# A decoder layer with 32 experts: 2 MB weight transfers, and residual rows gathered as input and as base of the result

## The reference, cut to what matters

```python
x  = x + merged @ w_out[l]                      # the residual rows, "x2" in the kernel
h2 = rms_norm(x, norm2_g[l])                    # x * rsqrt(mean(x*x) + EPS) * gain
# router: best of 4 groups, in that group the best 2 of 8 experts, with weights w
a  = xb @ w_gate[eid]; u = xb @ w_up[eid]       # xb: rows of h2 that chose the expert
y  = (silu(a) * u) @ w_down[eid]                # 1024 -> 512 -> 1024
out[token] = x[token] + sum over its two experts of w * y
```

## Time and profile before

| what | value |
|---|---|
| median of 3 runs | 1505.51 us (1505.3 to 1505.54) |
| the profiled execution, its own time | 1504.28 us |
| its span in the profile | 1502.3 us |
| PE / weight load of PE / DVE / ACT / POOL busy, share of span | 95 / 80 / 68 / 51 / 26% |
| granted clock of PE, mean | 0.988 |
| data moved | 282.68 MB |

### The profile page before, as it was taken

How to read it: one execution, slowest core, us unless ns; L and a number is a source line. 1 busy time by engine, 2 the same in 40 slices (tenths; PEclk the granted TensorE clock), 3 DMA queues, 4 the chain that set the end, 5 groups by cost and what they waited for, 6 DMA issues and landing times.

```text
span 1502.3 us, 19200 instructions
## 1 busy us (share of the span) xinstructions
PE 1431.3 (95%) x7296; PEld 1198.4 (80%) x7297; DVE 1015.5 (68%) x1433; ACT 768.6 (51%) x1091; POOL 387.9 (26%) x448
## 2 busy tenths in 40 slices
PE   5899999999999999999999969999999999999995
PEld 4788888888888788888888858888888787777784
DVE  6855655664664433434332876999999999999994
ACT  5643453453453322333232446767777777777772
POOL 2325325424424300000001421333332222222221
PEclk9999999999999999999999979999999999999998
DMA  7011010110210333453341469999999999999991
GB/s 227 13 43 45 17 43 11 51 42 2 60 43 1 85 84 89 122 144 85 84 189 57 169 234 377 362 373 376 375 378 375 374 367 364 367 370 368 365 347 49
DMA packets 129996, 282.68 MB, mean 188 GB/s; under 512 B 15728, under 2 KB 94704, under 8 KB 105328
## 3 DMA queue, kind: packets, MB, share of 16 engines
q1 hardware_dynamic: 119216, 264.31, 48.8%
q0 software_dynamic: 9216, 16.81, 4.5%
q10 hardware_dynamic: 1472, 0.32, 0.1%
HBM read 273.00 MB, written 25.17 MB: 198 GB/s over the span
## 4 chain that ended last, share of the span: by engine, by line
PE 72%; DMA 14%; DVE 6%; issue 2%; ACT 2%; POOL 2%; POOLq 0%; DVEq 0%; ACTq 0%
PE proj L105 14%; PE proj L107 14%; PE proj L106 13%; DMA w_slot<-in_w_up 9%; PE scores L105 5%; PE scores L107 5%; PE scores L106 5%; DMA w_slot<-in_w_gate 4%; PE outs L751 2%; PE scores L684 2%; DVE w_low L1703 2%; ACT w_high L1167 1%; PE turned L105 1%; PE turned L107 1%; PE turned L106 1%
## 5 line engine op out<-in xcount | busy, mean ns | idle before, releaser
L1703 DVE TENSOR_TENSOR w_low<-w_slot,w_high 128x2048 fp32r<-128x2048 f32 x192 | 434.4, 2285 | 11.1 <-ACT w_high L1167 10.0
L1167 ACT ACTIVATE w_high<-w_slot 128x2048 fp32r<-128x2048 f32 x190 | 359.6, 1914 | 106.7 <-DMA w_slot<-in_w_gate 40.8
L105 PE MATMUL proj<-w_high,xeH 128*128 128x512 f32 x512 | 206.2, 403 | 11.5 <-DVE w_low L1703 8.7
L107 PE MATMUL proj<-w_high,xeL 128*128 128x512 f32 x512 | 201.3, 393 | 0.0
L106 PE MATMUL proj<-w_low,xeH 128*128 128x512 f32 x512 | 201.2, 393 | 0.0
L1343 POOL DMA_INDIRECT out<-y,ids_rows x32 | 107.1, 3347 | 228.9 <-DVE y L1800 228.9
L105 PEld LDWEIGHTS proj<-w_high,xeH 128*128 128x128 f32 x512 | 97.2, 190 | 38.9 <-DVE w_low L1703 16.3
L975 ACT ACTIVATE wCH<-wC_in 128x1024 fp32r<-128x1024 f32 x48 | 47.6, 1052 | 154.4 <-DMA wC_in<-in_w_branch_b 154.4
L1398 DVE TENSOR_TENSOR wCL<-wC_in,wCH 128x1024 fp32r<-128x1024 f32 x48 | 56.9, 1237 | 91.3 <-ACT wCH L975 91.3
L107 PEld LDWEIGHTS proj<-w_high,xeL 128*128 128x128 f32 x512 | 97.1, 190 | 21.3
L1335 POOL DMA_INDIRECT xe<-h_rows,ids_rows x32 | 54.8, 1711 | 225.9 <-PE scores L562 213.4
(11 more groups left out here) (277 smaller groups left out, 3080.5 us busy)
## 6 DMA issues: line engine op xcount, KB each, us to landing
w_slot<-in_w_gate SPq DMA_DIRECT2D x64, 1024.0 KB, 21.1
w_slot<-in_w_up SPq DMA_DIRECT2D x64, 1024.0 KB, 22.2
w_slot<-in_w_down SPq DMA_DIRECT2D x64, 1024.0 KB, 21.1
wC_in<-in_w_in SPq DMA_DIRECT2D x32, 512.0 KB, 4.9
wB_in<-in_w_in SPq DMA_DIRECT2D x16, 512.0 KB, 6.4
wA_in<-in_w_in SPq DMA_DIRECT2D x12, 512.0 KB, 5.8
x_all<-in_x SPq DMA_DIRECT2D x4, 1024.0 KB, 8.7
wC_in<-in_w_branch_a SPq DMA_DIRECT2D x16, 256.0 KB, 5.6
```

The costliest lines, as they stand in the source:

```text
L105: pe.matmul(out, lh, rh, start=start, stop=False)
L107: return pe.matmul(out, ll, rh, start=False, stop=stop)
L1167: act.activation(w_high[slot][:], w_in6[slot][:], ACT.Copy).then_inc(S["w_split"], 1)
L1703: dve.tensor_tensor(w_low[slot][:], w_in6[slot][:], w_high[slot][:].bitcast(F32), ALU.subtract).then_inc(S["w_lows"], 1)
```

## The change

- Pieces c = 0, 1 are now the halves of gate, 2, 3 those of up. Two neighbouring pieces in slots (0,1), (4,5), (6,7) or (8,9) come by one 2 MB transfer, issued when both slots are used up, with one semaphore; slots 2 and 3 stay alone.
- The normalised rows are no longer made. x2 is stored twice, to a DRAM tensor and to the output; the experts gather x2 rows, into four buffers xe0 to xe3. After the transposes ACT applies the gain: eight activations of 128x128 with a scale per partition, into `xs`; then it rounds `xs` to xeH, and DVE subtracts in SBUF. 1/rms of a row is applied in silu (as scale) and in the row weight.
- The result is one instruction, y = product x weight + xe (residual row), in one buffer, and the scatter is a plain write. For a token's second expert the base must be the row as the first left it: DVE makes a second table `ids2_rows` (entries only for second experts), and POOL gathers these rows once more from the output (`gather_again`). y(e) waits for scatter e - 1, and from e = 4 for its second gather.
- The weight step is moved behind the first low halves (`weigh`) and grows from 7 to 15 DVE instructions; `weigh_rows` makes 96 columns for 32; silu(0) waits for three tables out of it.
- silu(e) waits for piece (e, 1) and no longer (e, 3); hid(e) waits for (e, 3).

```diff
+ALONE = (2, 3)
+def land_of(slot):
+    return f"w_land{slot if slot in ALONE else slot - slot % 2}"
...
+            def load_pair(q):
+                _, j, c = PIECES[q]
+                slot = q % N_SLOTS
+                if slot in ALONE:
+                    load_one(q)
+                    load_one(q + 1)
+                else:
+                    if q >= N_SLOTS:
+                        sp.wait_ge(S["w_used"], q - N_SLOTS + 2)
+                    sp.dma_start(w_pairs[slot][:, :, 0:2048], source(expert_at(j), c).rearrange("p (a b) -> p a b", a=2)
+                                 ).then_inc(S[land_of(slot)], DMA)
...
-            def x_high(value):
-                act.wait_ge(S["xeT_done"], value)
-                act.activation(xeH[:].rearrange("p a b -> p (a b)"), SC[:, 0, :], ACT.Copy).then_inc(S["xeH_done"], 1)
+            def x_scaled(turned, value, ks, count):
+                act.wait_ge(S[turned], value)
+                if count is not None:
+                    act.wait_ge(S["xeL_done"], count)
+                for k in ks:
+                    act.activation(xs[:, k, :], SC[:, 0, k * 128:(k + 1) * 128], ACT.Copy, scale=g2x[:, k:k + 1]).then_inc(S["xs_done"], 1)
+            def x_high(value, count=None):
+                x_scaled("xeT_done", value, range(8), count)
+                act.wait_ge(S["xs_done"], value * 8)
+                act.activation(xeH[:], xs[:], ACT.Copy).then_inc(S["xeH_done"], 1)
...
             def gate_silu(e):
-                act.wait_ge(S["w_used"], use_of(e, 3) + 1)
+                act.wait_ge(S["w_used"], use_of(e, 1) + 1)
                 act.wait_ge(S["hid_done"], e)
-                act.activation(silu[:], PROJ[0][:, :], ACT.Silu).then_inc(S["silu_done"], 1)
+                if e == 0:
+                    act.wait_ge(S["rows_weighed"], 3)
+                act.activation(silu[:], PROJ[0][:, :], ACT.Silu, scale=r_rows[:, expert_at(e):expert_at(e) + 1]).then_inc(S["silu_done"], 1)
...
-                if n == 0 and i >= 2:
-                    pool.wait_ge(S[f"h2_stored{i % 2}"], DMA * (i // 2))
-                pool.wait_ge(S["x2_done"], 8 * n + i + 1)
-                pool.tensor_tensor(h2[:, i % 2, cols], x2[:, i, cols], g2_row[:, cols], ALU.mult).then_inc(S["h2_gained"], 1)
...
+            for r in range(1, N_EXP + 1):
+                scatter_rows(r - 1)
+                if r + 3 < N_EXP:
+                    gather_rows(r + 3)
+                if N_GROUPS <= r + 1 < N_EXP:
+                    gather_again(r + 1)
...
             def rows_out(e):
                 dve.wait_ge(S["w_used"], use_of(e, 5) + 1)
...
-                dve.tensor_scalar(ys[e % 2][:], SC[:, 1, :], w_rows[:, expert_at(e):expert_at(e) + 1], None, ALU.mult
-                                  ).then_inc(S["y_out"], 1)
+                if e:
+                    dve.wait_ge(S["scattered"], DMA * e)
+                if e >= N_GROUPS:
+                    dve.wait_ge(S[f"again_landed{e % 2}"], DMA * ((e - N_GROUPS) // 2 + 1))
+                dve.scalar_tensor_tensor(y[:], SC[:, 1, :], w_rows[:, expert_at(e):expert_at(e) + 1], xe[e % 4][:], ALU.mult, ALU.add
+                                         ).then_inc(S["y_out"], 1)
```

More of the change, by code:

```diff
@@ L543, in _ @@
             sp.wait_ge(S["tables_done"], 2)
             def loads_again(n, e, b):
[L546 to L553, removed]
+                sp.wait_ge(S["scattered"], n * DMA + DMA * N_EXP)
@@ L554, in _ @@
+                for c in range(6):
+                    sp.dma_start(w_in6[BLOCK_SLOTS[c]][:], source(e, c)[:, c % 2 * 2048:c % 2 * 2048 + 2048]).then_inc(S["v_w"], DMA)
+            sp.wait_ge(S["scattered"], DMA * N_EXP)
             overflow(sp, loads_again)
-            sp.wait_ge(S["x2_stored"], N_TILES * DMA)
+            sp.wait_ge(S["out_stored"], N_TILES * DMA)
         def turn_rows(pe, src_rows, dst, step, n):
@@ L1187, in _ @@
             for half, turned, done in ((0, "x0_T", "x0_H"), (1, "xeT_done", "xeH_done")):
-                act.wait_ge(S[turned], 1)
-                act.activation(xeH[:, 4 * half:4 * half + 4, :].rearrange("p a b -> p (a b)"), bank(half), ACT.Copy
-                               ).then_inc(S[done], 1)
+                ks = slice(4 * half, 4 * half + 4)
+                x_scaled(turned, 1, range(4 * half, 4 * half + 4), None)
+                act.wait_ge(S["xs_done"], 4 * half + 4)
+                act.activation(xeH[:, ks, :], xs[:, ks, :], ACT.Copy).then_inc(S[done], 1)
             for c in (0, 1):
@@ L1213, in block_steps @@
                 act.wait_ge(S["w_used"], n * 6 + (6 * N_EXP + 4))
-                act.activation(silu[:], PROJ[0][:, :], ACT.Silu).then_inc(S["silu_done"], 1)
+                act.activation(silu[:], PROJ[0][:, :], ACT.Silu, scale=cur_r[:, 0:1]).then_inc(S["silu_done"], 1)
                 hid_high(n + (N_EXP + 1))
                 act.wait_ge(S["w_used"], n * 6 + (6 * N_EXP + 6))
-                act.activation(ys[0][:], SC[:, 1, :], ACT.Copy, scale=cur_w[:, 0:1]).then_inc(S["y_out"], 1)
-            for g in range(N_GROUPS):
-                act.wait_ge(S[f"scattered{g}"], DMA * (N_EXP // N_GROUPS))
+                act.activation(y[:], SC[:, 1, :], ACT.Copy, scale=cur_w[:, 0:1]).then_inc(S["y_out"], 1)
+            act.wait_ge(S["scattered"], DMA * N_EXP)
             overflow(act, block_steps)
@@ L1327, in _, with ids_of @@
             pool.wait_ge(S["lg_done"], 16)
[L1328 removed]
+            pool.memset(xe[0][:], 0.0).then_inc(S["xe_zero"], 1)
             pool.wait_ge(S["xe_zero"], 1)
[L1330 to L1331 removed]
+            pool.wait_ge(S["x2_stored"], N_TILES * DMA)
             pool.wait_ge(S["tables_done"], 1)
+            def ids_of(table, j):
+                return bass.IndirectOffsetOnAxis(ap=table[:, expert_at(j):expert_at(j) + 1], axis=0)
```

336 lines of the change are left out of this document (170 added, 166 removed).

## The result

The changed kernel is slower by a little: 1509.68 us, median of 8 runs (1507.09 to 1510.89), against 1505.20 for the kernel before beside it (8 runs, 1503.29 to 1506.73). Ratio 1.0031, 95% interval 1.0022 to 1.0041. The forecast was 1500 and faster.

What follows compares the result with a forecast made beforehand. Late experts were taken as bound by weight loads, above PE's 17.77 us; afterwards an ACT-DVE chain at 18.1. Terms -5.4 - 3.8 + 4.9 - 1.2 = -5.5 us gave 1498.8 profiled, 1500 median; range 1496 to 1504, with rivals 1488 to 1510.

Steps and rivals of the forecast that it cites:

- Part 2: 2 MB weight transfers: fewer issues count nothing; landing allowance falls from about 11 to 8 us, and just holds.
- Part 3: Expert loop, chain from turned rows over ACT's gains to xeL: period 18.1 us against 18.28, -5.4 us over 30 experts.
- Part 1: DMA work per expert: plain scatter outweighs second gathers, queue 58.2 us for 67.6, DMA-bound cost 18.06 to 18.36 from 18.65.
- rival C: Late experts: DMA engines still bind, at 18.65 us per expert, 8.5 us above the forecast, 1508.5 us; chance 0.14.
- Rival D: Weight loads: larger transfers make DMA so fast that no load is late; alone brings nothing more; no chance given.
- Part 4: Other waits in the loop, y for the previous scatter and POOL's second gathers: all hidden, nothing added.
- Part 5: Before the experts: without POOL's gain products DVE's conversions and picks run faster; -3.8 us (0 to -5).
- Part 6: Expert 0: gains before its first products, and silu(0) waiting for the row tables, cost +4.9 us (3 to 7).
- Part 7: End of kernel: the last scatter, without read and addition, lands 1.2 us sooner (0 to 1.5).

Runs made afterwards that it cites:

- a1: Changed kernel with the high half of piece (e+1, 1) put ahead of the next rows' gains on ACT: 1507.86 us, ratio 1.0018.
- a3: Changed kernel without the second gathers and without the waits for them: 1501.58 us, ratio 0.9976.
- a2: Changed kernel with every piece a 1 MB transfer again, issued when its own slot is used up: 1503.19 us, ratio 0.9991.
- a4: Changed kernel with an expert's rows spread over the partitions, first 64 places to even ones, others to odd: 1502.00 us, ratio 0.9983.
- b1: Kernel before with the scatters as plain writes, the addition left out: 1487.59 us, ratio 0.9885.
- b2: Kernel before with an expert's rows spread over the partitions, first 64 places to even ones, others to odd: 1488.29 us, ratio 0.9893.
- b3: b2 with the last two pieces' high halves ahead of silu(31) on ACT and low(31, 4) ahead of y(30) on DVE: 1482.44 us, ratio 0.9859.
- a8: Changed kernel with two 128x512 products per tile put back on POOL, into unused memory: 1509.86 us, ratio 1.0036.

## Why the prediction was wrong

The forecast for the span was -5.5 us, the profiled executions differ by +5.7. The 11.2 us between them, by its steps:

| step | forecast | came | missed |
|---|---|---|---|
| loop (parts 1 to 4) | -5.4 | +0.6 (iteration 1 to 30) | 6.0 |
| before the experts and expert 0 (5, 6) | +1.1 | +4.1 | 3.0 |
| end (7) | -1.2 | +1.0 | 2.2 |

The loop's 6.0 us are 4.8 of late periods (part 2), 0.7 for 18.12 where 18.10 stood, and 0.5 because the forecast counted a thirtieth iteration that lies behind the last turning. No single step explains the whole: without the late periods after would stand near 1504.9 us (1509.7 - 4.8), still not at 1500.

**Part 3 was right**, to 0.02 us a period: 18.12 for 18.10. a1 shows that it was this chain.

**Part 2 is the step that failed most**: "it just holds". The allowance was sized well: 19.1 us to landing where it binds, 11.0 at first, the 8 that I took. What used it up was the DMA work, taken as an average of 18.36 at most for all experts. The second gathers are not spread evenly: the first four experts have none, later ones ever more, as the order runs through each group from its first expert to its last. In after the queue of gathers and scatters moved 1.74 MB in the first four periods from 929 us, 2.38 MB in 1074 to 1146 and 3.02 MB in 1292 to 1364; in a3 the last of these is 2.25. The median landing of the 2 MB transfers grew accordingly, by 0.8 us from the first four periods to the next (10.0 to 10.8) and by 2.1 us between the stretches 1219 to 1291 and 1292 to 1364 (14.7 to 16.8). Work that rises to the end meets a buffer that is nearly spent; 4.8 us were lost in five periods. The 2 MB transfers, which I counted at nothing but 3 us of allowance, had a part in it: with 1 MB transfers (a2) the same work was never late. So had the second gathers (a3) and the rows in the first partitions (a4). Each of the three is needed for the loss, and none is the cause alone.

Part 1 was right as an average: the queue of gathers and scatters took 55.8 us for my 58.2, and leaving out the addition took 23.0 us from before for my 21.0. By the prediction's own sign, "a period that grows in the last experts", this is rival C, with 0.14, coming on top of the forecast's period instead of in its place. Rival D, that larger transfers make the DMA faster, has nothing for it: 387 GB/s against 385 where neither kernel is late. The 154 us that the prediction set against this, from the 2.0 us fixed per DMA in the Trainium skill (DMA: Bandwidth & Descriptors, "Anatomy of one DMA"), came from a section on DMAs that GpSimd issues, while SP issues these. No run here shows such a gain: a2, with 77 more of them than after, has the same early period, 18.12, and no late ones.

**Part 4** held: no wait for scatters or second gathers in the loop.

**Part 5** was right in mechanism and mis-sized in effect: -3.8 forecast; counted from DVE's first residual tile, 2.2 us came in the table of row numbers (72.86 for 75.02). I had added waits of PE for DVE as if each would come back whole. Between 835 and 855 us PE went from 18.79 us busy to 20.00, and is then the bound itself. In the table above stand another 0.4 us that belong to no part: in the profile of after the stage itself began that much later (809.14 for 808.77), which is within what varies from profile to profile.

**Part 6** was forecast at +4.9, and +5.9 came. Its first term was right: from the table to the first products of expert 0 are 9.63 us, before 8.32, so 1.3 for 1.25. Those products start 0.5 us earlier by the profiles (891.63 for 892.11) at the clock's lower level, 0.43 us from start to start, which lasts until 896.5 in both kernels; the turning in iteration 0 then comes 0.3 us later after their start (16.97 for 16.69 us). From that turning to the next there are 4.3 us more where 3.65 had been left (3.2 + 0.45). Two sizes were off there: the load of silu's table, 1.28 us, which had lain hidden at 899 before and wasn't counted, while the row tables were there 0.6 us sooner than worked out; and the clock, 0.7 us for my 0.45. After the 3.0 us wait for xeL the granted clock was 0.69 in 912 to 917 and 0.63 in 917 to 922 us. In the profile of before it was 0.69 and 0.97. In b1, b2 and b3, with the same instructions as before at this place, it stayed at 1.00, and iteration 0 to 1 took 14.6 instead of 16.20 us; so up to 1.6 us of what b2 gained over before is that and not the spread of the rows. Why it fell in before and not in them, no run shows.

**Part 7**: nothing came from the plain write in after. The shortest landing of a scatter fell from 5.9 to 3.2 us, but from the last scatter's issue to the end it is 8.93 us, before 8.79. The gain exists where there are no second gathers: it is 6.8 us in b1 (plain writes in before) and 6.6 in a3, so 2 us less, more than my 1.2. With the second gathers it is 8.8 to 8.95 in each of the other kernels made from after. How they hold up the end I haven't settled. The 1.0 us more go with the clock again, as far as the rows tell: PE's last 24 products ran at 0.58 (1490 to 1495 us) where before had 0.77 for the like stretch.

## What to carry to other kernels

When a buffer hides a resource that is slightly over its budget, don't multiply an average by the number of rounds: find in which rounds the work falls, and ask what is left of the buffer by then. A DMA share of 1.00 doesn't say that bytes are the bound; a few rows gathered into the first half of the partitions held up every weight transfer, and one table of places gained as much as leaving out the whole addition (1488.3 and 1487.6 us against 1505.2), with not a byte less to move. Before making transfers larger, check whether the queue ever runs dry: here it didn't, and the larger transfers only asked for more free space at once.

## What was not expected of the hardware

- With the accumulating scatter of 8.4 MB the queue's packets took 23.0 us more than with the plain one (67.6 against 44.6 us).
- Spreading some 64 rows over 128 partitions cut the landing of other transfers, queued at the same time, from 22.1 to 8.5 us, though the rows' own queue took more engine time (5.0% of 1484.3 us, 74 us, for 67.6).
- Eight activations of 128x128 with a scale per partition took 2.18 us together, 0.26 from start to start, though the page of the profile gives one of them 385 ns.
- DVE's conversion of 128x2 took 0.17 us alone and 0.95 beside a product of 128x512 on POOL (in a8 0.78).
